# The last feed-forward's second product as seven block products per quarter

## The reference, cut to what matters

```python
D_FF = 4 * D_MODEL                      # 4096, D_MODEL = 1024
h = rmsnorm(x, mlp_norm[l])
u = jnp.square(jax.nn.relu(jnp.einsum('bsd,df->bsf', h, w_ff1[l])))
x = x + jnp.einsum('bsf,fd->bsd', u, w_ff2[l])
...
return rmsnorm(x, final_norm)
```

## Time and profile before

| what | value |
|---|---|
| three runs | 2710.2, 2709.84, 2709.9 us, median 2709.9 |
| profiled execution: span of core 0, first to last instruction | 2708.0 us |
| the same against the median of the runs | 1.9 us less; no separate time of the profiled execution is given |
| instructions | 32235 |
| PE busy | 2687.0 us, 99% of the span |
| DVE, ACT, POOL busy | 1551.6, 1154.0, 681.2 us (57, 43, 25%) |
| DMA | 238.80 MB, mean 88 GB/s |
| granted TensorE clock | 1.000 |

### The profile page before, as it was taken

One profiled execution on the slowest core, in us unless ns is written; L12 is line 12 of the kernel. 1 busy time (PEld: TensorE's weight loads), 2 busy tenths in 40 slices (PEclk: granted clock), 3 DMA queues, 4 the chain that ended last, 5 costly groups with the idle time before them and its releaser, 6 DMA issues.

```text
span 2708.0 us, 32235 instructions
## 1 busy us (share of the span) xinstructions
PE 2687.0 (99%) x12902; PEld 2250.4 (83%) x12902; DVE 1551.6 (57%) x2312; ACT 1154.0 (43%) x1836; POOL 681.2 (25%) x695
## 2 busy tenths in 40 slices
PE   8999999999999999999999999999999999999999
PEld 7888888888888888888888888788888888788887
DVE  6656554344466646665575668644445558655444
ACT  4323423222347636532235767522224667522223
POOL 1000111011136626400004753411103553511100
PEclk9999999999999999999999999999999999999999
DMA  4332232323222222223322221233333211233332
GB/s 160 97 101 93 91 108 93 101 95 100 90 75 61 67 75 67 86 95 101 100 94 88 82 67 40 79 101 97 98 94 103 78 57 54 71 101 94 97 98 78
DMA packets 69414, 238.80 MB, mean 88 GB/s; under 512 B 7696, under 2 KB 10256, under 8 KB 69264
## 3 DMA queue, kind: packets, MB, share of 16 engines
q1 hardware_dynamic: 69264, 236.73, 28.1%
HBM read 234.60 MB, written 2.10 MB: 87 GB/s over the span
## 4 chain that ended last, share of the span: by engine, by line
PE 91%; DVE 4%; POOL 2%; ACT 2%; issue 0%; DMA 0%; SPq 0%; ACTq 0%; DVEq 0%
PE ps L416 29%; PE ps L418 29%; PE ps L417 29%; POOL wl L2419 2%; PE ps L552 1%; PE ps L777 1%; PE ps L776 1%; PE ps L485 0%; DVE wl L1636 0%; ACT wh L1018 0%; PE ps L613 0%; PE ps L612 0%; DVE xl L1648 0%; PE ps L470 0%; PE ps L452 0%
## 5 line engine op out<-in xcount | busy, mean ns | idle before, releaser
L1018 ACT ACTIVATE wh<-raw 128x1024 fp32r<-128x1024 f32 (+2 forms) x453 | 465.2, 1028 | 730.7 <-PE ps L418 723.7
L416 PE MATMUL ps<-xh,wh 128*128 128x512 f32 x1920 | 751.7, 391 | 0.2 <-POOL wl L2419 0.2
L418 PE MATMUL ps<-xh,wl 128*128 128x512 f32 x1920 | 747.4, 389 | 0.0
L417 PE MATMUL ps<-xl,wh 128*128 128x512 f32 x1920 | 747.2, 389 | 0.0
L1636 DVE TENSOR_TENSOR wl<-raw,wh 128x1024 fp32r<-128x1024 f32 (+1 forms) x339 | 447.7, 1321 | 156.9 <-ACT wh L1018 156.5
L416 PE MATMUL ps<-yh,wh 128*128 128x512 f32 x1088 | 425.3, 391 | 1.9 <-POOL wl L2419 1.9
L416 PEld LDWEIGHTS ps<-xh,wh 128*128 128x128 f32 x1920 | 360.5, 188 | 76.2 <-issue 1.0
L417 PE MATMUL ps<-yl,wh 128*128 128x512 f32 x1088 | 423.5, 389 | 0.0
L418 PE MATMUL ps<-yh,wl 128*128 128x512 f32 x1088 | 423.4, 389 | 0.0
L418 PEld LDWEIGHTS ps<-xh,wl 128*128 128x128 f32 x1920 | 360.4, 188 | 75.1
L417 PEld LDWEIGHTS ps<-xl,wh 128*128 128x128 f32 x1920 | 360.6, 188 | 74.8 <-issue 1.0
(11 more groups left out here) (267 smaller groups left out, 3628.6 us busy)
## 6 DMA issues: line engine op xcount, KB each, us to landing
raw<-in_ff SPq DMA_DIRECT2D x120, 512.0 KB, 3.6
raw<-in_pool_in SPq DMA_DIRECT2D x64, 512.0 KB, 3.3
raw<-in_conv_in SPq DMA_DIRECT2D x64, 512.0 KB, 3.3
raw<-in_pool_out SPq DMA_DIRECT2D x32, 512.0 KB, 3.3
raw<-in_qk SPq DMA_DIRECT2D x32, 512.0 KB, 3.7
raw<-in_pool_grp SPq DMA_DIRECT2D x16, 512.0 KB, 3.3
raw<-in_conv_out SPq DMA_DIRECT2D x16, 512.0 KB, 3.3
raw<-in_mla_z SPq DMA_DIRECT2D x16, 512.0 KB, 3.6
```

The costliest lines, as they stand in the source:

```text
L416: pe.do.matmul(o, lh, rh_, start=start, stop=False)
L417: pe.do.matmul(o, lh, rl_, start=False, stop=False)
L418: return pe.do.matmul(o, ll, rh_, start=False, stop=stop)
L1018: act.do.activation(h[:, 0:ncol], r[:, 0:ncol], ACT.Copy).then_inc(*mark("whi", ("whi", k)))
```

## The change

Only the last feed-forward (l = 1) is changed, in all four quarters.

- The quarter's product of 512 tokens by 1024 rows by 1024 columns is cut in 2 x 2 x 2 blocks and made of seven block products (`PRODUCTS`) in the place of eight, by a scheme with four sums of blocks on each side. Each product is 256 tokens by 512 rows by 512 columns: two units of 12 matmuls (`zq`), with tokens as rows. Q1, Q2, Q3 read `yh`, `yl`; W5, Q6, Q7, Q4 read the token-side sums `tt0` to `tt3`. The products run in three chains of two banks each: A (Q1, Q6, Q7, Q4), C (W5, Q3) and B (Q2). Within a chain a product goes on in the bank of the one before, and PE waits until DVE has added the earlier state of it to `x` (`zp`).
- Token side: the squares go from POOL to ACT (`ff_square`), the first product's units run in the order 0, 4, 1, 5, 2, 6, 3, 7, and after each pair DVE makes four sums of 128 by 256 (`t_sums`), ACT and DVE split the 128 by 1024 of them (`t_high`, `t_low`).
- Weight side: S1 and S3 are made by transfers that add into SBUF, issued by GpSimd in halves of 64 partitions (`weight_sum`); S2 and S4 by DVE (`wsum`). SP loads the four blocks and the base of S1 (`pieces`).
- `x` is transposed in quarter 0 (`turn_x`), four banks behind the fifth unit and four behind the sixth, and the blocks lie in `x0` to `x7` from then on (`zblock`). Each product ends in two additions on DVE (`post`). The last norm is woven into the last products.

The core of the diff:

```diff
+FF_ORDER = (tuple(range(8)), (0, 4, 1, 5, 2, 6, 3, 7))
+PRODUCTS = ("Q1", "W5", "Q6", "Q2", "Q7", "Q3", "Q4")
+PIECES = (("A11", 0, 0), ("A21", 1, 0), ("A12", 0, 1), ("A22", 1, 1))
+WEIGHT_OF = {"Q1": "A11", "W5": "S1", "Q6": "S2", "Q2": "A12", "Q7": "S3", "Q3": "S4", "Q4": "A22"}
+CHAIN_OF = {"Q1": "A", "W5": "C", "Q6": "A", "Q2": "B", "Q7": "A", "Q3": "C", "Q4": "A"}
+CHAIN_BEFORE = {"Q6": "Q1", "Q7": "Q6", "Q4": "Q7", "Q3": "W5"}
+CHAIN_LAST = ("Q2", "Q3", "Q4")
+POST = {"Q1": (0, 0, 1), "W5": (1, 1, -1), "Q6": (0, 1, 1), "Q2": (0, 0, 1), "Q7": (1, 1, -1), "Q3": (0, 1, 1),
+        "Q4": (1, 0, -1)}
+POST_BEFORE = {"Q2": "Q1", "Q7": "W5", "Q3": "Q6"}
+ROWS_Y = {"Q1": (0, 0), "Q2": (4, 0), "Q3": (4, 256)}
+ROWS_T = {"W5": 0, "Q6": 1, "Q7": 2, "Q4": 3}
...
+                for name in PRODUCTS:
+                    for kk in range(2):
+                        add(("zq", qd, name, kk), (qd, name, kk), 1024)
...
+                    for n in range(2 if qd == 0 else 0, 8):
+                        xgemm(st + 1, "f1", l, qd, order[n], norm=st + 1 if qd == 0 and n == 3 else None)
+                        if l == 1 and qd == 0 and n in (4, 5):
+                            turn_x(n - 4)
...
+            def turn_x(half):
+                for tb in range(4):
+                    b = bank("ox", tb, half)
+                    for i in range(4):
+                        m = half * 4 + i
+                        pe.wait_ge(*at("x", 7, m))
+                        mm = pe.do.transpose(b[:, i * 128:i * 128 + 128], x[m][:, tb * 128:tb * 128 + 128], ident)
+                    mm.then_inc(*mark("group", ("mm", "ox", tb, half)))
...
+            def quarter(qd):
+                for name in PRODUCTS:
+                    ns = [unit["zq", qd, name, kk] for kk in range(2)]
+                    chain, before = CHAIN_OF[name], CHAIN_BEFORE.get(name)
+                    if before is None:
+                        for tb in range(2):
+                            bank("z" + chain, qd, tb)
+                    steps = [(kk, kp, tb) for kk in range(2) for kp in range(2) for tb in range(2)]
+                    if qd == 3 and name == "Q4":
+                        steps = [(kk, kp, tb) for tb in range(2) for kk in range(2) for kp in range(2)]
+                    for kk, kp, tb in steps:
+                        wh, wl = unit_ready(ns[kk])
+                        k = 2 * kk + kp
+                        if k == 0 and before is not None:
+                            pe.wait_ge(*at("zp", qd, before, tb))
+                        if name in ROWS_Y:
+                            y0, c0 = ROWS_Y[name]
+                            pe.wait_ge(*at("yl", "f21", qd, y0 + k))
+                            tc = slice(c0 + tb * 128, c0 + tb * 128 + 128)
+                            th, tl = YH[y0 + k][:, tc], YL[y0 + k][:, tc]
+                        else:
+                            c0 = ROWS_T[name] * 256 + tb * 128
+                            pe.wait_ge(*at("ttl", qd, k))
+                            th, tl = TT[k][:, c0:c0 + 128], TT[k][:, 1024 + c0:1024 + c0 + 128]
+                        o = ps("z" + chain, qd, tb)
+                        cc = slice(kp * S, kp * S + S)
+                        if before is None:
+                            mm = mm3(o[:, :], th, tl, wh[:, cc], wl[:, cc], k == 0, k == 3)
+                        else:
+                            mm = mm3_on(o[:, :], th, tl, wh[:, cc], wl[:, cc], k == 3)
+                        done = [("mm", "zq", qd, name, tb)] if k == 3 else []
+                        if kp == 1 and tb == 1:
+                            done.append(("wfree", ns[kk]))
+                        if done:
+                            mm.then_inc(*mark("group", *done))
 
...
+                def turned_in(half):
+                    act.wait_ge(*at("mm", "ox", 3, half))
+                    for i in range(4):
+                        act.wait_ge(*at("xl", 7, 4 * half + i))
+                    for tb in range(4):
+                        act.do.activation(zblock(half, tb), ps("ox", tb, half)[:, :], ACT.Copy).then_inc(
...
+                        if n and n % 2 == 0:
+                            t_high(qd, n // 2 - 1)
+                        ff_square(qd, i)
+                        ff_high(qd, i)
+                        if qd == 0 and n in (5, 6):
+                            turned_in(n - 5)
...
+            def last_rows(name, kk):
+                if name == "Q7":
+                    row_square(0, kk, 16)
+                elif name == "Q3":
+                    row_square(1, 2 + kk, 16)
+                elif name == "Q4":
+                    row_square(0, 2 + kk, 20)
+                    row_scale(0, 2 + kk)
...
+                def t_sums(qd, k):
+                    y, y4 = temp("ff", l, qd, k), temp("ff", l, qd, k + 4)
+                    t1, t2, t3, t4 = [TS[:, 256 * n:256 * n + 256] for n in range(4)]
+                    dve.wait_ge(*at("ffs", l, qd, k + 4))
+                    dve.do.tensor_tensor(t1, y[:, 0:256], y[:, 256:512], ALU.subtract).then_inc(
+                        *mark("dve", ("t1n", qd, k)))
+                    dve.do.tensor_tensor(t3, y4[:, 256:512], y[:, 256:512], ALU.subtract)
+                    dve.wait_ge(*at("t1n", qd, k))
+                    dve.do.scalar_tensor_tensor(t2, t1, -1.0, y4[:, 256:512], ALU.mult, ALU.subtract).then_inc(
+                        *mark("dve", ("t2n", qd, k)))
+                    dve.wait_ge(*at("t2n", qd, k))
+                    dve.do.scalar_tensor_tensor(t4, t2, -1.0, y4[:, 0:256], ALU.mult, ALU.subtract).then_inc(
+                        *mark("dve", ("tsum", qd, k), ("tfree", "ff", l, qd, k), ("tfree", "ff", l, qd, k + 4)))
+
+                def t_low(qd, k):
+                    low(TT[k][:, 1024:2048], TS[:, :], TT[k][:, 0:1024], ("tth", qd, k), ("ttl", qd, k))
+
+                def wsum(qd, name, kk, a, b):
+                    cc = slice(kk * 1024, kk * 1024 + 1024)
+                    dve.wait_ge(*at("wsrc", qd, a, kk))
+                    dve.wait_ge(*at("wsrc", qd, b, kk))
+                    dve.do.tensor_tensor(RB[name][:, cc], RB[a][:, cc], RB[b][:, cc], ALU.add).then_inc(
+                        *mark("dve", ("wsrc", qd, name, kk)))
...
+                def quarter(qd):
+                    for n, name in enumerate(PRODUCTS):
+                        for kk in range(2):
+                            taking("zq", qd, name, kk)
+                            if n:
+                                post(qd, PRODUCTS[n - 1], kk)
+                            if name == "Q1":
+                                wsum(qd, "S2", kk, "S1", "A11")
+                            if name == "Q6":
+                                wsum(qd, "S4", kk, "S2", "A12")
+                            if qd == 3 and name in ("Q3", "Q4"):
+                                row_first(0 if name == "Q3" else 1, kk if name == "Q3" else 2 + kk)
+                    if qd == 3:
+                        row_second(0, 2)
+                        row_second(0, 3)
+                    for tb in range(2):
+                        post(qd, "Q4", tb)
+                        if qd == 3:
+                            row_second(1, tb)
+
...
+                        if l == 1 and n and n % 2 == 0:
+                            t_sums(qd, n // 2 - 1)
+                        weights(unit["f1", l, qd, i] + AHEAD[min(n, 4) if qd == 0 else 4])
+                        if l == 1 and n and n % 2 == 0:
+                            t_low(qd, n // 2 - 1)
+                        if qd or n == 7:
                             ff_low(qd, i)
...
+                def weight_sum(qd, name, first, second, kk):
+                    pool.wait_ge(*at(*first))
+                    for half in range(2):
+                        rows = slice(64 * half, 64 * half + 64)
+                        pool.do.dma_start(RB[name][rows, kk * 1024:kk * 1024 + 1024], second[rows, :],
+                                          accum_op=ALU.add).then_inc(
+                            *mark(f"ff2{name}{kk}", *([("wsrc", qd, name, kk)] if half else []), by=16))
...
+            def pieces(qd):
+                for kk in range(2):
+                    if qd:
+                        sp.wait_ge(*at("wlo", unit["zq", qd - 1, "W5", kk]))
+                        sp.wait_ge(*at("wsrc", qd - 1, "S2", kk))
+                    else:
+                        sp.wait_ge(*at("mm", "pv", 1, "d", 3))
+                    sp.do.dma_start(RB["S1"][:, kk * 1024:kk * 1024 + 1024], D["ff2t"][qd, 1, 0, kk]).then_inc(
+                        *mark(f"ff2base{kk}", ("wbase", qd, kk), by=16))
+                    for name, half, rows in PIECES:
+                        if qd:
+                            if name in ("A11", "A12"):
+                                sp.wait_ge(*at("wsrc", qd - 1, "S4", kk))
+                            sp.wait_ge(*at("wlo", unit["zq", qd - 1, {"A11": "Q6", "A12": "Q3", "A21": "Q7",
```

(6 more changed lines are left out.)

282 lines of the change are left out of this document (157 added, 125 removed).

## The result

The changed kernel takes **2720.66 us** (median of 4, 2720.22 to 2721.75) against 2709.87 (4 runs, 2709.69 to 2710.2): 1.004 times the time, 95% interval 1.0026 to 1.0054, so slower by 0.4%. Its profiled execution spans 2718.5 us at a mean clock of 0.995.

A forecast was written before the change was run, and what follows sets the result against it. PE was taken as the bound. The terms sum to +10.2 us, taking the profiled span from 2708.0 to 2718.2 us; with 1.9 us for the median, the forecast is 2720.1 us, range 2715.3 to 2728 (chance 0.65).

The forecast's parts named there:

- 96 matmuls: All four quarters: seven products of 24 matmuls replace eight units of 24, each matmul 0.227 us on PE, -21.8 us.
- transposes in rows: PE's 32 transposes stay but cost less done in one go than as groups between units, -0.9 us.
- ahead of the sixth unit: Quarter 0: the first transposes wait for DVE to empty the third unit's bank, +1.7 us.
- E to the seventh unit: Quarter 0: after the sixth unit's end (E), full banks put the seventh unit's start at 13.5 us, not 1.5, +12.0 us.
- slow starts behind it: Quarter 0: after PE's long wait, eight matmuls start at twice the distance, half clock, +1.8 us; bounds 0 and 3.6.
- turn, quarter 0: Quarter 0, after the eighth unit's end (T): PE waits on DVE, ACT's weight split 1.55 us later, +4.2 us.
- turns, quarters 1 to 3: After each eighth unit's end (T): PE waits for W5's second half and Q6's second bank, 2.7 us each, +8.0 us.
- wait at Q4's second half: From Q2 on, DVE's work per half unit stays below PE's 2.72 us, so no wait was found: 0.
- the end: From PE's last matmul to the end: DVE and ACT have four rows left, 11.2 us against 6.0, +5.2 us.
- Costs of nothing: Squares on ACT, squares gone from POOL, SP's loads and GpSimd's adding transfers (estimated 2.6 us each) were taken to cost nothing.
- The queues keep up: Rival: DVE is past the fourth and fifth emptying before the sixth unit's end, waits go, 2692.4 us; chance 0.12.
- only the turn is hidden: Rival: DVE's pieces after the eighth unit's end fit, 8.0 and part of 4.2 us go, 2710 us; chance 0.16.

The follow-up runs named there:

- the kernel with all edits: The changed kernel with first-quarter split table and ACT copies moved earlier, the turn between products reordered and the last rows reordered on DVE and ACT: 2689.27 us.
- the run with the copy moved up: The changed kernel with only ACT's four copies of the first transposed half moved from behind the sixth unit's square and split to behind the fourth's: 2713.67 us.
- the kernel with the turn reordered: The changed kernel with DVE's S2 additions, W5's second weight half and Q1's additions placed earlier in the queues between first and second product: 2709.85 us.

## Why the prediction was right, point by point

The forecast was 2720.1 us and a span of 2718.2; it came out at 2720.66 and 2718.5. Term by term, from matmul starts (a wait is the distance of starts less 0.227):

| term | predicted | measured |
|---|---|---|
| 96 matmuls | -21.8 | -21.8 |
| transposes in rows | -0.9 | 0 |
| ahead of the sixth unit | +1.7 | +1.7 |
| E to the seventh unit | +12.0 | +11.7 |
| slow starts behind it | +1.8 | +1.4 |
| turn, quarter 0 | +4.2 | +4.1 |
| turns, quarters 1 to 3 | +8.0 | +7.4 |
| wait at Q4's second half | 0 | +1.1 |
| the end | +5.2 | +4.7 |
| sum | +10.2 | +10.3 (spans: 10.5) |

The mechanism was right in the main: where PE waits, for whom, and about how long. That the sum meets the measured time to 0.6 us is in part luck. Five terms were 0.1 to 0.6 us too large, 1.9 us together, and two were wrong by 2.0 us the other way: the gain on the transposes, which doesn't exist, and the wait at Q4's second half, which the prediction put at nothing.

*The bound and the removed matmuls.* PE has 12806 matmuls against 12902. With the waits gone PE runs through this stretch, and the kernel with all edits is 20.6 us faster than the one before: 21.8 less some 1.1 us of a longer tail (7.3 against 6.2). So matmuls that go do count in full.

*Transposes.* Sixteen in one go take 1.67 us from the first to the next unit and 0.08 in its first start, so two sets take 3.5. Eight groups of four took 0.35 + 0.09 each, 3.5 too, so there is no gain in a row. The term came from two readings: 1.5 us for a set where it is 1.75, and some 0.5 us for a group between units, from 47.5 less 43.5 us. The first of these windows holds two matmuls of 512 columns more than the second (227 less 32 transposes is 195, against 193), which is 0.45 of the 4.0 us.

*The banks.* The links of the chain came out one by one: DVE's weight half at E + 1.34 (1.36 in the text), emptied banks at E + 4.30 and E + 5.24 (4.37, 5.3), the sixth unit's at E + 10.8 (11.0), the seventh unit at E + 13.4 (13.5). The experiments show what the sum could only argue: two faults of order in series, 15 us together with what hangs on them.

*The clock.* It fell as foreseen: the starts are 0.2 us late each until 2402, and the transposes before them take longer too. But the turn's term in quarter 0 is **right in size and wrong in make-up**. I had a wait of 2.95 at W5's second half (1.4 + 1.55) and 1.3 at Q6. The wait was 2.4, Q6 waited for nothing, and 1.7 us went into slow starts from 2422.22 on, which I had not foreseen. They gave DVE the time that Q6 would have waited for: in the run with the copy moved up the slow starts are missing, and there Q6 waits in quarter 0 too:

```profile
PE ps L460 <- DVE x L2486: 2.8, 4, 0.7
```

That turn cost 3.7 us there, against 4.1 here.

*The turns of quarters 1 to 3.* W5's second half stands at T + 9.37 (9.56 in the text), 1.3 us late with its first start; Q6's second bank 1.15 us. Two waits, the releasers named, three times.

*The end.* 4.7 for the last rows (5.2) and 1.1 us that I left out, at Q4's second weight half. The prediction has "From Q2 on [...] I find no wait", reckoned from DVE's work in a half unit, and this is the step that failed. In quarter 3 a weight's low half, an addition on DVE, a square on ACT and the next weight's high half wait for one another from Q7 on. DVE's low halves then start at 2691.63, 2695.20, 2698.76 and 2702.33, 3.57 us apart, where PE takes 2.72 for a half unit. I had looked for waits of PE in the tail's queues only behind its last matmul.

*Costs of nothing.* Adding transfers: confirmed (+0.2 us without them), but not by their price. They land after 4.3 us in the median and not after the estimated 2.6, and eight of them take about 37 us in the first quarter and not 27. Squares on ACT: confirmed, and more: with the squares on GpSimd the kernel is 5.5 us slower. In the kernel before DVE's weight halves take 1.48 us in the mean in this stretch, and 1.22 after the change.

*Rivals.* "The queues keep up" and "only the turn is hidden" describe the reordered kernels, not this one. 2710 was written for the second, and the kernel with the turn reordered takes 2709.9. 2692.4 was written for the first, with 5.2 us for the end; the kernel with all order edits takes 2689.3, and its end costs 1.1.

## What to carry to other kernels

When work that bounds is shortened, look in the queues of the other engines for an item that waits for the bound engine and has ready work behind it: the price of such a place is found by walking the queue from the event it waits for, and here it was right to 0.6 us at each place that was walked. The one place whose queue was not walked, Q4's second half, hid 1.1 us. The releaser that a wait names is only the last cause; undo each of two in a run of its own and both together before one is blamed. Then repair the order before the idea is given up: the same instructions gave 2720.7 and 2689.3 us.

## What the runs showed of the hardware that was not expected

**Slow starts don't follow from a wait's length alone.** The wait of 2.27 or 2.28 us at the turn of quarter 0 stands in six of these kernels. In five, seven or eight distances between starts behind it are 0.43 us, the lower of the two levels, 1.2 GHz. In the one with the copy moved up there is none. Its granted clock was 0.68 around the transposes behind the wait of 4.2 us, and 1.00 around the wait of 2.27 (stretch, length, then as in the earlier trace rows):

```profile
2391.00:2396.00 5.00, 4.75 (x23) 4.49 (x24) 3.41 (x9) 4.46 (x8) 0.81 (x1) 0.68 0.49 82
2414.00:2421.00 7.00, 4.30 (x17) 3.02 (x18) 7.00 (x8) 3.18 (x3) 0.81 (x1) 1.00 0.41 89
```

Behind the equal wait of 5.45 us in four of the kernels five to nine distances are 0.43 us. Waits of 0.7 to 1.75 us never brought them; one of 2.40 and one of 2.73 did. The Trainium skill (TensorE: Matmul & The Clock Gate, section What's actually happening) says of a kernel's start that the number of slow matmuls varies from run to run with where the activity falls in the gate's own count of time; these runs agree in the middle of a kernel, with none against seven behind equal waits. What decides it was not tested here. So a wait of over 2 us on PE may bring 1.7 us of slow starts beyond itself, and may not; at this turn they cost only some 0.5 us in the end, since PE would have waited at Q6 otherwise.

**An adding transfer of 256 KB lands after 4.3 us in the median, and one of 128 KB after 4.2**; GpSimd's queue holds the next one back for the most part of that behind each whole one, and behind each one to three of the halves.
